# Three of the eight low halves made on GpSimd behind chunk 0 of a hybrid decoder step

## What is computed

```python
h = rms_norm(x, lw['norm_mix'])
u = h @ lw['w_in']
u_r, u_f, u_g = jnp.split(u, [D_SHIFT, D_SHIFT + D_FOX_IN], axis=-1)
o_r, new_shift, new_wkv = rwkv_time_mix(u_r, shift_prev, wkv0, lw)
q, k, v, f_logit = jnp.split(u_f, [D_FOX, 2 * D_FOX, 3 * D_FOX], axis=-1)
o_f = attend(q, k, v, lf)
merged = jax.nn.sigmoid(g_r) * (o_r @ lw['w_br_rwkv']) + jax.nn.sigmoid(g_f) * (o_f @ lw['w_br_fox'])
x = x + merged @ lw['w_out']
h2 = rms_norm(x, lw['norm_ffn'])
x = x + jnp.square(jax.nn.relu(h2 @ lw['w_ffn_up'])) @ lw['w_ffn_down']
```

## Time and profile before

| | us |
|---|---|
| median of 3 timed runs | 2015.66 (2012.57, 2015.66, 2017.42) |
| the profiled execution's own time | 2009.9 |
| its span | 2007.8 |
| TensorE busy | 1931.1 (96%) |
| VectorE busy | 1144.4 (57%) |
| ScalarE busy | 707.2 (35%) |
| GpSimd busy | 272.0 (14%) |

### The profile page before, as it was taken

The page is one execution under the profiler, slowest core; times in us unless marked ns, Lnnn a source line. Parts: engine busy times, 40 slices in busy tenths (PEclk is TensorE's granted clock), DMA queues, the critical chain, the costliest instruction groups (busy, mean ns, idle before and its releaser), DMA issues.

```text
span 2007.8 us, 40418 instructions
## 1 busy us (share of the span) xinstructions
PE 1931.1 (96%) x16234; PEld 1788.5 (89%) x16234; DVE 1144.4 (57%) x1810; ACT 707.2 (35%) x1183; POOL 272.0 (14%) x244
## 2 busy tenths in 40 slices
PE   7999999999999998999998999999999999999997
PEld 7998579999999998975667999899999999999996
DVE  6556766666666665337776654867666543233334
ACT  5114442322333333144455533644444331111113
POOL 0000112222222221222110000112121100000000
PEclk9999999999999999999999999999999999999998
DMA  4212812222233324665555641042323352222212
GB/s 178 84 42 87 294 25 60 61 53 60 61 83 104 104 78 141 172 208 187 188 191 172 218 132 53 27 122 88 119 92 99 114 192 95 85 85 97 84 42 87
DMA packets 122218, 224.13 MB, mean 112 GB/s; under 512 B 64006, under 2 KB 67366, under 8 KB 120758
## 3 DMA queue, kind: packets, MB, share of 16 engines
q1 hardware_dynamic: 119766, 213.49, 33.9%
q10 hardware_dynamic: 2304, 8.50, 1.3%
HBM read 167.00 MB, written 54.96 MB: 111 GB/s over the span
## 4 chain that ended last, share of the span: by engine, by line
PE 70%; issue 14%; DVE 9%; ACT 2%; DMA 2%; POOL 1%; SPq 1%; DVEq 0%; ACTq 0%; POOLq 0%
PE ps L349 27%; PE ps L1517 10%; PE ps L1527 6%; PE ps L441 5%; PE ps L443 4%; PE ps L442 4%; PE ps L1138 2%; PE ps L1139 1%; PE ps L1169 1%; PE ps L1430 1%; PE ps L1444 1%; DVE arena L2197 1%; DVE arena L2190 1%; PE ps L1460 1%; POOL w_fill_low L646 1%
## 5 line engine op out<-in xcount | busy, mean ns | idle before, releaser
L349 PE MATMUL ps<-ff_tiles_a,wb_split 128*128 128x350 f32 (+1 forms) x1422 | 231.4, 323 | 0.6 <-DVE ff_tiles_a L2633 0.6
L349 PEld LDWEIGHTS ps<-ff_tiles_a,wb_split 128*128 128x128 f32 x1422 | 228.8, 189 | 1.2 <-DVE ff_tiles_a L2633 0.8
L2533 DVE TENSOR_TENSOR arena<-arena,ps 128x1050 f32<-128x1050 f32 x39 | 48.7, 1249 | 270.2 <-PE ps L349 270.1
L2760 POOL TENSOR_TENSOR arena<-arena,constants 64x512 f32<-64x512 f32 x100 | 121.7, 1217 | 333.0 <-DVE arena L2190 323.1
L1517 PE MATMUL ps<-t_halves,s_halves 128*128 128x350 f32 x960 | 162.5, 326 | 3.9 <-issue 3.7
L361 ACT CAST wb_split<-weights 128x1024 fp32r<-128x1024 f32 x56 | 58.5, 1045 | 302.0 <-PE ps L349 297.5
L1517 PEld LDWEIGHTS ps<-t_halves,s_halves 128*128 128x128 f32 x960 | 156.9, 190 | 5.1 <-issue 4.9
L443 PE MATMUL ps<-fill_high,w_fill_low 128*128 128x350 f32 x468 | 152.3, 326 | 0.0
L1138 PE MATMUL ps<-arena 64*64 64x64 f32 x1600 | 113.2, 220 | 10.7 <-DVE arena L2220 5.3
L1138 PEld LDWEIGHTS ps<-arena 64*64 64x64 f32 x1600 | 101.2, 134 | 24.6 <-issue 15.0
L349 PE MATMUL ps<-h_high,w_split 128*128 128x350 f32 (+1 forms) x576 | 115.2, 332 | 2.9 <-DVE w_split L365 2.9
(11 more groups left out here) (390 smaller groups left out, 4251.7 us busy)
## 6 DMA issues: line engine op xcount, KB each, us to landing
weights<-in_wu SPq DMA_DIRECT2D x122, 512.0 KB, 4.1
normed<-in_vp SPq DMA_DIRECT2D x64, 260.0 KB, 4.7
normed<-in_kp SPq DMA_DIRECT2D x64, 256.0 KB, 5.1
arena<-chunk_dram SPq DMA_DIRECT2D x10, 1248.0 KB, 6.9
ff_tiles_a<-ff_dram SPq DMA_DIRECT2D x20, 524.0 KB, 5.5
arena<-gate_dram SPq DMA_DIRECT2D x16, 525.0 KB, 4.1
ff_dram<-squares SPq DMA_DIRECT2D x16, 524.0 KB, 3.9
ff_dram<-arena SPq DMA_DIRECT2D x16, 524.0 KB, 3.5
```

What stands on the lines that cost most here:

```text
L349: last = pe.matmul(PS[:, 3 * s + g, 0:n], ws[s][wh][:, k * P:(k + 1) * P], tile_of(x[xh], k)[:, g * G:g * G + n], start=(k == 0 and wh + x ...
L2533: dve.tensor_tensor(dst, dst, grp(s), ALU.add).then_inc(evac[s], 1)
L2760: ch_pool.done(pool.tensor_tensor(Bm[lv % 2][part, :, 0:n], MB[part, :, 0, part], mask.unsqueeze(1).to_broadcast([n, NH, n]), ALU.mult), f ...
```

## The change

VectorE makes the lows of k = 0 to 4 (HL_DVE = 5), GpSimd those of k = 5 to 7, in its own copy of chunk 0 between the mask products and the bonus. GpSimd waits for the same two conditions as VectorE (all high copies made, chunk 0's filler through). Its lows are counted by a semaphore of their own, hl_made_p, and the filler of chunk 1 waits for the one or the other according to k. GpSimd's loop begins with chunk 1. The arithmetic of each low is unchanged.

```diff
--- before.py
+++ after.py
@@ -416,7 +416,7 @@
         class Filler:
 
 
-            def __init__(self, pe, v, ns=0, first=None):
+            def __init__(self, pe, v, ns=0, first=False):
                 self.pe, self.v, self.ns, self.first = pe, v, ns, first
                 late = [*range(NS, KT), *range(NS)] if ns or first else list(range(KT))
                 self.left = [(s, g, i, k) for s in range(2) for g in range(NG)
@@ -433,8 +433,11 @@
                             self.pe.wait_ge(w_in[s], 16 * self.v + 16)
 
                         self.pe.wait_ge(sub_read, 2 * NG * self.v + (m + 1 - 2 * NG * V_FOX0))
-                    if m == 0 and self.first is not None and k < NS:
-                        self.pe.wait_ge(self.first, k + 1)
+                    if m == 0 and self.first:
+                        if k < HL_DVE:
+                            self.pe.wait_ge(hl_made, k + 1)
+                        else:
+                            self.pe.wait_ge(hl_made_p, k + 1 - HL_DVE)
                     out, w = PS[:, 6 + m % 2, 0:G], W[:, s, k * P:(k + 1) * P]
                     if k < self.ns:
                         wl_ = WL[:, s, k * P:(k + 1) * P]
@@ -625,7 +628,8 @@
         WL = own("w_fill_low", w_at, 2, D, dtype=F32R)
         assert r_ch.at <= GT_at and wf_at + NS * P <= ar_end
         wf_high, wf_done = [sem("wf_high0"), sem("wf_high1")], [sem("wf_done0"), sem("wf_done1")]
-        hf_made, hl_made = sem("hf_made"), sem("hl_made")
+        hf_made, hl_made, hl_made_p = sem("hf_made"), sem("hl_made"), sem("hl_made_p")
+        HL_DVE = 5
         y_stored, y_in = sem("y_stored"), sem("y_in")
 
         def fill_w(s, k):
@@ -1112,7 +1116,7 @@
                 ch_pe.done(last, "yt")
 
             def pe_chunk(c):
-                fill = Filler(pe, c + V_FOX0, NS, hl_made if c == 1 else None) if c else fill0
+                fill = Filler(pe, c + V_FOX0, NS, c == 1) if c else fill0
 
                 def wait(steps, name):
                     pe.wait_ge(steps.sem, steps.after(c, name))
@@ -2267,7 +2271,7 @@
             dve_chunk(0, early=False)
             dve.wait_ge(hf_made, NS)
             dve.wait_ge(unit_done, 2 * V_FOX0 + 2)
-            for k in range(NS):
+            for k in range(HL_DVE):
                 dve.tensor_tensor(HL[:, k], HT[:, k, :], HF[k], ALU.subtract).then_inc(hl_made, 1)
             with dve.Fori(1, NC - 1) as c:
                 dve_chunk(c)
@@ -2749,7 +2753,7 @@
         def _(pool):
 
             pool.sem_inc(ch_pool.sem, 1)
-            with pool.Fori(0, NC) as c:
+            def pool_chunk(c):
                 pool.wait_ge(ch_dve.sem, ch_dve.after(c, "mask_b1"))
                 for lv in LEVELS[:-1]:
                     if lv > 2:
@@ -2761,11 +2765,20 @@
                                                         mask.unsqueeze(1).to_broadcast([n, NH, n]), ALU.mult),
                                      f"bm_{lv}_{name}")
                         pool.wait_ge(ch_pool.sem, ch_pool.after(c, f"bm_{lv}_{name}"))
+                if isinstance(c, int) and c == 0:
+                    pool.wait_ge(hf_made, NS)
+                    pool.wait_ge(unit_done, 2 * V_FOX0 + 2)
+                    for k in range(HL_DVE, NS):
+                        pool.tensor_tensor(HL[:, k], HT[:, k, :], HF[k], ALU.subtract).then_inc(hl_made_p, 1)
                 pool.wait_ge(bg_in, 16 * c + 16)
                 pool.wait_ge(ch_act.sem, ch_act.after(c, f"y_{HP - 1}"))
                 ch_pool.done(pool.tensor_tensor(YTc, YTc, BGc[:, 0:HP], ALU.add), "bonus")
                 pool.wait_ge(ch_pool.sem, ch_pool.after(c, "bonus"))
                 ch_pool.done(pool.tensor_tensor(YTc, YTc, BGc[:, HP:2 * HP], ALU.mult), "gate")
+
+            pool_chunk(0)
+            with pool.Fori(1, NC) as c:
+                pool_chunk(c)
 
             fill_split_low(pool, NC, 1)
             for i in range(NC + 1, PV_FILL):
```

## The result

| | kernel before | changed kernel |
|---|---|---|
| median, us | 2013.93 (2009.47 to 2019.49, 20 runs) | 2018.61 (2015.5 to 2024.39, 20 runs) |
| ratio to before | | 1.0021, 95% interval 1.0013 to 1.0029 |
| the same in a second session | 2013.35 (35 runs) | 2016.75 (12 runs), 1.0017 (1.0004 to 1.0030) |
| profiled span, us | 2007.8 | 2014.1 |

The change makes the kernel slower, by 2.6 to 5.8 us by the first interval; 5.9 us had been forecast. The chain of work that ended last is mostly TensorE's as before (82% with 3% of "issue" here, 70% with 14% in the earlier trace rows; VectorE 9% in both), and in the chunk loop TensorE is as busy as in the earlier trace rows.

A forecast was written before the change was run, and what follows sets the result against it. TensorE was taken to bound the kernel (70% of the chain that ended last). Filler +6.3 us less 0.4 regained gives +5.9; 2015.7 + 5.9 = 2021.6 us, range 2016.5 to 2024.

The forecast's parts named there:

- Two paths of equal length start in the lows: Chunk 1: TensorE's filler (297.28) and VectorE's step "k" (297.34) end together; shortening one alone wins nothing, lengthening either loses.
- The two engines take turns, whole instructions, the waiting one next: Lows of chunk 1: three GpSimd turns of 2.31 us cost 6.9 and save 3.5; VectorE's part ends at 295.4, not 292.33.
- queued lows: Rival at chunk 1's lows: VectorE's queued lows keep their turn; some +3.6 us net, 2019.3 us; chance 0.12.
- no mutual hold: Rival at chunk 1's lows: the engines hardly block each other; -1.0 us, 2014.7 us, measuring as the same; chance 0.11.
- The clock: TensorE, chunk 1's filler: gaps drop it to 1.2 GHz until 5.3 us after k=3; filler +6.3 us, without low clock +4.1.
- VectorE's path, 5.0 us behind the last low: Chunk 1, last low to end of step "k": 5.0 us, so "k" is ready at 300.4, ahead of TensorE.
- 0.4 us come back: Chunk 1, behind the filler: 0.34 us between L1122 and first mask product, and some of 0.11 before L1122, are regained.
- The loss goes to the end whole: Rest of the chunk loop: next to no slack on TensorE (49.04 of 50 us busy), so the loss reaches the end nearly whole.

The follow-up runs named there:

- f: Kernel before, VectorE making two of its eight lows in its wait ahead of the norm step: 0.9998, again 0.9995 of the kernel before.
- k: Changed kernel, but GpSimd makes only the first low, early, behind VectorE's squares step; VectorE the other seven behind its norm step: 1.0001 of the kernel before.
- c: Changed kernel, VectorE's five lows reading one operand from PSUM instead of SBUF (values not the reference's): 1.0012 of the kernel before.
- e: Changed kernel with 36 and 11 extra matmuls into an unused bank in TensorE's two long gaps: 1.0028 of the kernel before.
- d: Changed kernel, GpSimd waiting for VectorE's fifth low before starting its three: 1.0027 of the kernel before.
- b: Changed kernel with only one low on GpSimd and seven on VectorE: 1.0020, again 1.0004 of the kernel before.
- l: Changed kernel, but GpSimd makes one low early behind the squares step, VectorE one ahead of its norm step and six behind: 0.9989 of the kernel before.

## Why the prediction was right, step by step

- *Two paths of equal length start in the lows.* Held in part. Lows that are ready earlier win as much as the last of them is earlier, within 0.2 us (f, k). But there both paths get their lows earlier at once; that shortening one of them alone wins nothing was not tried.
- *The two engines take turns, whole instructions, the waiting one next.* Held to the instruction: the order was the one played out, with the norm step at 2.90 (2.9 forecast), two lows of VectorE at 3.33 and 3.45 (3.4), turns of 1.11 (1.11) and 2.26 us (2.31). The fifth low ended 294.21 - 274.91 = 19.30 us behind "sum", 3.01 later than the eighth before (292.33 - 276.04 = 16.29); 3.08 was forecast. c shows it to be the cause: without VectorE's second SBUF operand the shift is +0.24. The rivals of queued lows and of no mutual hold fall with the same rows. The Trainium skill ("SBUF — State Buffer", "SBUF: two separate sides") limits the hold to VectorE operations with two SBUF inputs or in a two-port mode. The traces agree: in c five lows take 5.88 us beside GpSimd, and in k the reduction keeps its 0.69 us beside GpSimd; no run here tries the two-port mode.
- *The clock.* Its mechanism held, its size was too large. It fell earlier than thought (283.58 - 274.91 = 8.7 us behind "sum", where before it was 286.24 - 276.04 = 10.2), and came back 297.24 - 293.10 = 4.1 us after k=3, not 5.3. The filler's end moved by (301.88 - 274.91) - (297.28 - 276.04) = 5.73 us where 6.3 was forecast. e puts the low clock's part of the loss at 1.4 us.
- *VectorE's path, 5.0 us behind the last low.* It took 6.1 ("k" ends 25.42 us behind "sum", the last low 19.30): the first scan waits 0.97 us for y_back, a wait that the prediction did not name. TensorE still came last (26.81), so it cost nothing.
- *0.4 us come back.* They did: +5.73 at the filler's end, +5.46 at L1126, +5.12 at the first mask product. But by the next chunk's "sum" the shift was +5.54 (67.52 us against 61.98 behind the first), and +5.82 at the end of the loop. This term of the sum was wrong: the time came back and was lost again, inside chunk 1 and little by little in the chunks behind it. Inside chunk 1 the traces show one step. Up to the second pair of VectorE's level steps (L2220, now L2224) the shift is +5.22; there the pair of the kernel before (first row) runs through, and in the changed kernel the second of the two waits 0.48 us for TensorE's level products, and behind it the shift is +5.58:

```profile
313.81 0.96 DVE L2220 TENSOR_TENSOR arena<-arena,ps 104x256 f32<-104x256 f32 x2 [0.57 <-PE ps L1139]
```

```profile
317.90 0.42 DVE L2224 TENSOR_TENSOR arena<-arena,ps 104x256 f32<-104x256 f32 x1 [0.57 <-PE ps L1143]
318.81 0.42 DVE L2224 TENSOR_TENSOR arena<-arena,ps 104x256 f32<-104x256 f32 x1 [0.48 <-PE ps L1143]
```

(Timelines of the kernel before and of the changed kernel, chunk 1.) The same wait stands in the changed kernel's second execution and in c, d and e, which all lose 0.40 to 0.42 us between the first mask product and chunk 1's "sum"; b has neither. Why TensorE is late there, and what is lost behind chunk 1, stays open. The forecast put the filler's end 0.6 us too late and let 0.5 us too much come back; the two errors cancel, and that the net of 5.9 is so near 5.82 is partly luck.
- *The loss goes to the end whole.* It does to the end of the loop. Behind it the executions spread over 10.4 us, and the two timings, +2.6 to +5.8 and +0.8 to +6.0, leave open whether all of 5.8 arrives or 2 us of it are made up. The time on the clock was 2018.6 where 2021.6 was forecast, of which 1.7 us are the kernel before itself, whose median over 20 runs is 2013.93 and not 2015.66.

## What to carry to other kernels

Work handed from VectorE to GpSimd counts by the turns that it takes from VectorE's own operations with two SBUF operands: here 2.3 us per low against 1.165 saved, so each low on GpSimd lost as much as it was to win, and the engine's low busy share said nothing about that. Look instead for a stretch in which VectorE waits or reduces one operand: there the same operation on GpSimd gained 1.1 us (k), and VectorE's own waiting time held two lows for a gain of 1.7 to 1.9 (f). Beside VectorE operations that read one operand from PSUM there was no turn to pay either (c). And count the gap on TensorE ahead of the first product too: 1.4 of the 5.1 us were its clock.

None of the tried orders is shown to be faster than the kernel before by its time; f, k and l are 1.2 to 1.9 us ahead by their traces up to the end of the loop.

## What had not been expected of the hardware

Scans of 104 columns wait their turn like the lows and the norm step (1.84 and 2.40 us instead of 0.38), and so does a product of a tile with itself (2.16 instead of 0.69). By these rows the recorded start of such an instruction is the moment at which it begins to wait, on GpSimd as on VectorE (a low starts 0.04 us behind the end of the one before it and lasts 3.33 us), so that the recorded durations of both engines overlap though the work does not: VectorE's five lows and the norm step are recorded with 2.90 + 10.19 us, where their turns alone make 6.3.
